# Expert weights through twelve ring slots and four staging slots that ScalarE and GpSimd empty by copies

## The reference, cut to what matters

```
g   = softmax(t @ rg_w + rg_b)             # one group of 4 is taken
e   = softmax(expert logits in the group)  # two experts of 8 are taken
hg, hu = t @ w_gate[e], t @ w_up[e]        # 2048 -> 512, for 32 experts
out = sum over chosen e of comb * ((silu(hg) * hu) @ w_down[e])   # 512 -> 2048
x   = LN2(alpha * x + gate2 * out)
```

## Time and profile before

| what | value |
|---|---|
| runs shown | 1637.08 us median of 3 (1636.77 to 1637.81) |
| the profiled execution | 1640.42 us |
| its span in the profile | 1638.6 us, 22796 instructions |
| TensorE (PE) busy | 1521.7 us, 93% |
| DVE, ScalarE (ACT), GpSimd (POOL) busy | 507.6, 253.9, 142.0 us |
| SP's queue, q1 | 510.20 MB, 78.4% of 16 engines over the span |
| chain that ended last | PE 78%, DMA 14%, DVE 3%, ACT 2% |

### The profile page before, as it was taken

The page is one execution under the profiler, slowest core; times in us unless marked ns, Lnnn a source line. Parts: engine busy times, 40 slices in busy tenths (PEclk is TensorE's granted clock), DMA queues, the critical chain, the costliest instruction groups (busy, mean ns, idle before and its releaser), DMA issues.

```text
span 1638.6 us, 22796 instructions
## 1 busy us (share of the span) xinstructions
PE 1521.7 (93%) x8535; PEld 659.9 (40%) x8536; DVE 507.6 (31%) x1446; ACT 253.9 (15%) x540; POOL 142.0 (9%) x215
## 2 busy tenths in 40 slices
PE   3999999999999899899999999999999999999974
PEld 2557555456344444433333333333333333333321
DVE  6468334323133246742111121212121121211216
ACT  2220000033122322112111110101010000000111
POOL 6001000041020140000000000000000000000011
PEclk9999899999799899799999999999999999999997
DMA  9995778883267869989999979999799999999965
GB/s 297 376 386 195 254 266 301 295 246 112 75 237 295 319 222 398 411 352 423 422 422 421 421 291 422 421 421 422 301 407 422 421 421 421 422 421 422 421 238 221
DMA packets 119288, 559.70 MB, mean 342 GB/s; under 512 B 15657, under 2 KB 20553, under 8 KB 64921
## 3 DMA queue, kind: packets, MB, share of 16 engines
q1 hardware_dynamic: 100800, 510.20, 78.4%
q0 software_dynamic: 17952, 46.05, 8.4%
q10 hardware_dynamic: 482, 2.70, 0.6%
HBM read 565.78 MB, written 42.37 MB: 371 GB/s over the span
## 4 chain that ended last, share of the span: by engine, by line
PE 78%; DMA 14%; DVE 3%; ACT 2%; issue 1%; POOL 0%; SPq 0%; POOLq 0%; DVEq 0%; ACTq 0%
PE bank L791 23%; PE bank L808 11%; DMA ring<-in_exp_w_up 10%; PE bank L2378 6%; PE bank L753 5%; PE bank L2286 5%; PE bank L2135 3%; PE bank L347 3%; DMA ring<-in_ada_w 3%; PE bank L2218 2%; PE bank L2329 2%; PE bank L760 2%; DMA ring<-in_w_in 2%; DVE BC L609 1%; PE bank L2113 1%
## 5 line engine op out<-in xcount | busy, mean ns | idle before, releaser
L791 PE MATMUL bank<-ring,BC 128*64 128x512 f32 x1984 | 473.4, 596 | 5.6 <-DMA ring<-in_exp_w_up 3.2
L791 PEld LDWEIGHTS bank<-ring,BC 128*64 128x64 f32 x1984 | 150.2, 137 | 301.8 <-issue 280.4
L808 PE MATMUL bank<-ring,BC 128*64 128x512 f32 x992 | 219.7, 595 | 16.7 <-ACT BC L714 16.7
L588 DVE COPY MOD<-bank 128x512 f32<-128x512 f32 x32 | 22.1, 692 | 430.2 <-PE bank L760 430.2
L753 PE MATMUL bank<-H,MOD 128*64 128x512 f32 x512 | 132.9, 592 | 0.3 <-DVE H L1995 0.3
L808 PEld LDWEIGHTS bank<-ring,BC 128*64 128x64 f32 x992 | 70.8, 137 | 142.5 <-issue 142.5
L544 POOL DMA_INDIRECT y_dram<-BC,y_row x31 | 29.9, 965 | 947.2 <-DVE y_row L618 862.1
L2378 PE MATMUL bank<-ring,MT 128*128 128x512 f32 x224 | 101.7, 607 | 1.0 <-issue 0.8
L702 ACT COPY MOD<-bank 128x512 f32<-128x512 f32 x32 | 18.7, 585 | 461.6 <-PE bank L760 461.6
L2286 PE MATMUL bank<-ring,MT 128*128 128x512 f32 x192 | 85.9, 600 | 1.0 <-ACT X L1211 1.0
L615 DVE COPY BC<-bank 128x512 f32<-128x512 f32 x31 | 21.4, 691 | 166.1 <-PE bank L808 166.1
(11 more groups left out here) (560 smaller groups left out, 1459.0 us busy)
## 6 DMA issues: line engine op xcount, KB each, us to landing
ring<-in_exp_w_gate SPq DMA_DIRECT2D x128, 1024.0 KB
ring<-in_exp_w_up SPq DMA_DIRECT2D x128, 1024.0 KB
ring<-in_exp_w_down SPq DMA_DIRECT2D x128, 1024.0 KB
ring<-in_ada_w SPq DMA_DIRECT2D x96, 1024.0 KB
ring<-in_w_in SPq DMA_DIRECT2D x20, 1024.0 KB
y_dram<-con POOLq DMA_DIRECT2D x20, 1024.0 KB, 34.2
ring<-in_w_out SPq DMA_DIRECT2D x16, 1024.0 KB
ring<-in_ssm_glu_w SPq DMA_DIRECT2D x4, 1024.0 KB
```

The lines of the kernel that those rows point to most:

```text
L791: mm = pe.matmul(bank[64 * i:64 * i + 64, 2, :], xT[:, q // 2, k % 4, 64 * (q % 2):64 * (q % 2) + 64], ring[:, at, 512 * (k % 4):512 * (k ...
L808: mm = pe.matmul(bank[64 * (c % 2):64 * (c % 2) + 64, 4 + c // 2, :], aT[:, j, :], ring[:, at, 512 * c:512 * c + 512], start=(j == 0), sto ...
```

## The change

Four more slots of one chunk, 12 to 15, are added to the ring. They take the place of memory that was `MT` and `GE`: slots 12 and 13 and the start of 14 lie in `MT`, the rest of 14 and slot 15 in `GE`. `HF` and `DW` move to other places for it. For every expert from 1 on, down chunk 8 to 11 is fetched into slot 12 to 15, before the expert's gate and up chunks. When TensorE has used the down chunk of the block before, an engine copies the staged chunk into its ring slot: ScalarE chunks 8 and 9, POOL chunks 10 and 11, POOL's one before and one after the scatter. Where the next block is of the same expert, the copy reads and writes the ring slot itself: the source is chosen by a register (`step`, 0 or 1, from a new part of `rint`). A staging slot may be filled again when the copy for the first block of the expert before has been made. TensorE waits for the copies instead of the landings. For expert 1 the order is 8, 9, 0, 1, 10, 11, 2 to 7, with a wait for `x1_ready` 2 ahead of chunk 10, as `GE` is in use until then. The DW products move to the start of DVE's tail. POOL's body for the block after the last also makes its two copies, and ScalarE waits for them before `y_all`.

```diff
--- before.py
+++ after.py
@@ build @@
+    stage_of = {j: RING + i for i, j in enumerate(STAGED)}
...
-        ring = sb("ring", [P, RING, 2048])
+        slots = sb("slots", [P, RING * 2048 + 2 * D + KD * T])
+        ring = slots[:, 0:(RING + len(STAGED)) * 2048].rearrange("p (s n) -> p s n", n=2048)
+        MTf, GEf = slots[:, RING * 2048:RING * 2048 + KD * T], slots[:, RING * 2048 + KD * T:]
...
-        DW = MTf[:, 2560:3328].rearrange("p (b i n) -> p b i n", b=3, i=2)
+        DW = BCf[:, 0:768].rearrange("p (b i n) -> p b i n", b=3, i=2)
...
+        def copy_staged(eng, copy, done, e, j, step, place):
+            at, to = slot_of[j], stage_of[j]
+            eng.wait_ge(used, len(plan) + (e - 1) * RING + j + 1)
+            eng.wait_ge(landed[at], 16 * (last_slot_uses[at] + 1) + 16 * place)
+            copy(ring[:, at:at + 1, :], ring[:, at:to + 1:to - at, :][:, bass.ds(step, 1), :]).then_inc(done, 1)
...
@@ moe_pool @@
             def body(e):
-                pool.wait_ge(S("rint_ready"), since("rint_ready") + 4)
+                step = pool.value_load(rint[0:1, bass.ds(e + (I_STEP - 1), 1)], min_val=0, max_val=1)
+                place = pool.value_load(rint[0:1, bass.ds(e + I_PLACE, 1)], min_val=0, max_val=E - 1)
+                copy_staged(pool, nc.gpsimd.tensor_copy, S("copied_pool"), e, 10, step, place)
+                pool.wait_ge(S("rint_ready"), since("rint_ready") + 5)
                 pool.wait_ge(S("y_row"), e)
                 pool.indirect_dma_start(...)
+                copy_staged(pool, nc.gpsimd.tensor_copy, S("copied_pool"), e, 11, step, place)
@@ moe_sp @@
-            with sp.Fori(1, E) as e:
+            def fetch(e, expert, before, j):
+                if j in STAGED:
+                    name, n = copies_of(j)
+                    sp.wait_ge(S(name), since(name) + before * 2 + n + 1)
+                    load_expert_chunk(sp, expert, j, live > e, stage_of[j])
+                    return
+                load_expert_chunk(sp, expert, j, live > e)
...
+            for j in (8, 9, 0, 1, 10, 11, 2, 3, 4, 5, 6, 7):
+                if j in STAGED:
+                    if j >= 10:
+                        sp.wait_ge(S("x1_ready"), 2)
+                else:
+                    sp.wait_ge(used, len(plan) + (first - 1) * RING + j + 1)
+                fetch(1, expert, 0, j)
+            with sp.Fori(2, E) as e:
                 first = sp.value_load(rint[0:1, bass.ds(e + I_FIRST, 1)], min_val=1, max_val=NBLK - 1)
+                before = sp.value_load(rint[0:1, bass.ds(e + (I_FIRST - 1), 1)], min_val=0, max_val=NBLK - 1)
                 expert = sp.value_load(rint[0:1, bass.ds(e + I_LIST, 1)], min_val=0, max_val=E - 1)
-                for j in range(RING):
-                    sp.wait_ge(used, len(plan) + (first - 1) * RING + j + 1)
-                    load_expert_chunk(sp, expert, j, live > e)
+                for j in [*STAGED, *range(8)]:
+                    if j < 8:
+                        sp.wait_ge(used, len(plan) + (first - 1) * RING + j + 1)
+                    fetch(e, expert, before, j)
@@ moe_dve, after the integer table's first four parts @@
+            go(V.tensor_scalar(places, bank[0:1, 3, 0:NBLK], E - 1.0, None, ALU.min))
+            V.tensor_tensor(rint[0:1, I_STEP:I_STEP + NBLK - 1], places[:, 1:], places[:, 0:NBLK - 1], ALU.subtract)\
+             .then_inc(S("rint_ready"), 1)
...
-            for b in range(3):
-                for i in range(2):
-                    V.tensor_scalar(DW[:, b, i, :], ident, cwt[:, b, i:i + 1], None, ALU.mult).then_inc(S("dw_ready"), 1)
@@ moe_act, body @@
                 turned_out(e + 1)
+                for j in (8, 9):
+                    copy_staged(act, nc.scalar.copy, S("copied_act"), e + 1, j, step, place)
                 act.wait_ge(used, len(plan) + (e + 1) * RING)
...
+            act.wait_ge(S("copied_pool"), 2 * (extra + FULL) + since("copied_pool") + 2)
             act.wait_ge(S("y_written"), 16 * (extra + FULL) + Y_FILLED)
@@ moe_pe, body @@
                     at = slot_of[8 + j]
-                    pe.wait_ge(landed[at], 16 * (last_slot_uses[at] + 1) + 16 * place)
+                    name, n = copies_of(8 + j)
+                    pe.wait_ge(S(name), since(name) + e * 2 + n + 1)
@@ tail_dve @@
+            for b in range(3):
+                for i in range(2):
+                    V.tensor_scalar(DW[:, b, i, :], ident, cwt[:, b, i:i + 1], None, ALU.mult).then_inc(S("dw_ready"), 1)
             dve.wait_ge(S("g2_ready"), 5)
```

More of the change, by code:

```diff
@@ L52 @@
 RING = 12
+STAGED = range(8, 12)
+STAGE_ACT = 2
 QC = 4
@@ L79 @@
 I_EXTRA, I_PLACE, I_LIST, I_FIRST = 0, 1, 1 + NBLK, 1 + 2 * NBLK
-I_LIVE, I_N = I_FIRST + E, I_FIRST + E + 1
+I_LIVE, I_STEP = I_FIRST + E, I_FIRST + E + 1
+I_N = I_STEP + NBLK
 def constants():
@@ L190 @@
     "slots_ready": ("sel_ready", 3),
-    "x_first": ("sel_ready", 4),
+    "copied_act": ("qs_ready", 8),
+    "copied_pool": ("glu_sig", 8),
 }
@@ L254, in build @@
         ones = con[:, C_ONE:C_ONE + P]
-        later = ring[:, 6:12, :].rearrange("p a b -> p (a b)")
+        later = slots[:, 6 * 2048:12 * 2048]
         Hf = H[:, :, :].rearrange("p a b -> p (a b)")
@@ L548, in body @@
                     .then_inc(S("y_written"), 16)
-            pool.wait_ge(S("rint_ready"), since("rint_ready") + 4)
+                copy_staged(pool, nc.gpsimd.tensor_copy, S("copied_pool"), e, 11, step, place)
+            for j in (10, 11):
+                pool.wait_ge(landed[slot_of[j]], 16 * (last_slot_uses[slot_of[j]] + 1))
+                pool.nop().then_inc(S("copied_pool"), 1)
+            pool.wait_ge(S("rint_ready"), since("rint_ready") + 5)
             expert_loops(pool, body, 1)
@@ L556, in moe_sp @@
             live = sp.value_load(rint[0:1, I_LIVE:I_LIVE + 1], min_val=1, max_val=E)
-            with sp.Fori(1, E) as e:
+            def fetch(e, expert, before, j):
[5 more added lines that the diff above has]
+                load_expert_chunk(sp, expert, j, live > e)
+            first = sp.value_load(rint[0:1, I_FIRST + 1:I_FIRST + 2], min_val=1, max_val=NBLK - 1)
+            expert = sp.value_load(rint[0:1, I_LIST + 1:I_LIST + 2], min_val=0, max_val=E - 1)
+            for j in (8, 9, 0, 1, 10, 11, 2, 3, 4, 5, 6, 7):
[6 more added lines that the diff above has]
+            with sp.Fori(2, E) as e:
                 first = sp.value_load(rint[0:1, bass.ds(e + I_FIRST, 1)], min_val=1, max_val=NBLK - 1)
+                before = sp.value_load(rint[0:1, bass.ds(e + (I_FIRST - 1), 1)], min_val=0, max_val=NBLK - 1)
                 expert = sp.value_load(rint[0:1, bass.ds(e + I_LIST, 1)], min_val=0, max_val=E - 1)
-                for j in range(RING):
-                    sp.wait_ge(used, len(plan) + (first - 1) * RING + j + 1)
-                    load_expert_chunk(sp, expert, j, live > e)
+                for j in [*STAGED, *range(8)]:
+                    if j < 8:
+                        sp.wait_ge(used, len(plan) + (first - 1) * RING + j + 1)
+                    fetch(e, expert, before, j)
             tail_sp(sp)
@@ L657, in moe_dve @@
             V.tensor_copy(rint[0:1, I_EXTRA:I_EXTRA + 1], behind[0:1, 0:1]).then_inc(S("rint_ready"), 1)
-            V.tensor_copy(rint[0:1, I_LIVE:I_N], behind[0:1, 1:2]).then_inc(S("rint_ready"), 1)
+            V.tensor_copy(rint[0:1, I_LIVE:I_STEP], behind[0:1, 1:2]).then_inc(S("rint_ready"), 1)
             V.tensor_scalar(rint[0:1, I_PLACE:I_FIRST], bank[0:1, 3, 0:2 * NBLK], E - 1.0, None, ALU.min)\
@@ L709, in body @@
             def body(e):
+                step = act.value_load(rint[0:1, bass.ds(e + I_STEP, 1)], min_val=0, max_val=1)
+                place = act.value_load(rint[0:1, bass.ds(e + (I_PLACE + 1), 1)], min_val=0, max_val=E - 1)
                 rows_out(e + 1)
@@ L720, in moe_act @@
             act.nop().then_inc(S("ys_act"), 1)
+            for j in (8, 9):
+                act.wait_ge(landed[slot_of[j]], 16 * (last_slot_uses[slot_of[j]] + 1))
+                act.nop().then_inc(S("copied_act"), 1)
             rows_out(0)
@@ L726, in moe_act @@
             nc.scalar.activation(rsm[:, 3, :, 0:1], rsm[:, 3, :, 0:1], ACT.Exp).then_inc(S("lg_exp"), 1)
-            act.wait_ge(S("rint_ready"), since("rint_ready") + 4)
+            act.wait_ge(S("rint_ready"), since("rint_ready") + 5)
             extra = expert_loops(act, body)
+            act.wait_ge(S("copied_pool"), 2 * (extra + FULL) + since("copied_pool") + 2)
             act.wait_ge(S("y_written"), 16 * (extra + FULL) + Y_FILLED)
```

15 lines of the change are left out of this document (7 added, 8 removed).

## The result

The changed kernel takes **1649.81 us** (median of 6 runs, 1644.63 to 1653.31), the kernel before in the same session 1636.92 (6 runs, 1635.76 to 1638.2): ratio 1.0082, interval 1.006 to 1.0103. So it is slower by 12.9 us on the medians; the forecast was 18.2 us more than 1637. The profiled execution took 1649.46 us with a span of 1647.7.

A forecast was written before the change was run, and what follows sets the result against it. TensorE was taken to set the pace at 28.15 us a block, with 14.7 us of waits for weights. Start 8.6, copies 3.0 and 3.2, end 3.4 gave +18.2 us; on the median 1637.08 that is 1655.3, taken as 1655, range 1646 to 1666.

The forecast's parts named there:

- B: Behind the two double blocks (one expert filling two blocks), the DMA waits for POOL's copy of chunk 11: 3.0 and 3.2 us.
- C: At the end, POOL's last copy lies wholly on the path to the first gather: +3.4 us.
- the copies are of another length: Sign of being wrong: POOL's copies in the profile after do not take about 3.1 us each.
- What bounds the kernel: In the expert loop TensorE sets the pace, 28.15 us a block; 14.7 us are waits for weights.
- The dips: Two falls in the GB/s row, 291 and 301, where no slot is given back; forecast to stay as deep.
- The fast rival: The holes at the double blocks are filled, both losses (1.6 and 13.1 us) vanish: 1625.8 us; chance 0.07.
- Term A: At the start, expert 2's gate/up chunks come later by two chunks net (5.1 us) and a dry stretch: +8.6 us.
- Waits and small parts: nothing: TensorE's waits for copies, the new integer operations, the value_loads and the moved DW products cost nothing.
- B1: Ahead of the second double block, the wait for POOL's copy behind the first one costs 3.0 us.
- B2: Behind the second double block, where the lead is already spent, the wait for POOL's copy costs 3.2 us.
- The likeliest case: The forecast itself for the whole kernel: +18.2 us, taken as 1655 us; chance 0.65.
- Half of it: Rival: the start costs only 5.1 us and POOL copies in 1.8 us: 10.7 us slower, 1648; chance 0.10.

The follow-up runs named there:

- gate16: Against the kernel before: sixteen slots, no copies, only chunks 0 to 3 of an expert have two places each; 1640.2 us, ratio 1.0018.
- a_late: The changed kernel with ScalarE's two waits moved from ahead of its first row copies to just ahead of the loop; 1646.19 us, ratio 1.0052.
- a_act4: a_late with ScalarE making all four copies and POOL none; 1650.33 us, ratio 1.0089.
- the ring of sixteen: Against the kernel before: sixteen slots as one ring in fetch order, no copies, TensorE's body standing four times; 1657.19 us, ratio 1.0131.

## Why the prediction was right, and where only its sum was

Direction and range were right, the range in part by luck. Of the terms one held roughly, one was put at nothing and cost 5.7 us at the start, and two (B and C) were far too large. One of the prediction's own signs of being wrong also came true: the copies are of another length.

- **What bounds the kernel, and that the slots bring nothing in steady state**: right. The dips stayed, the losses behind block 17 stayed, and the first loss came near block 5, as forecast. (In the earlier trace rows slice 30 has 407, which the reading "flat at 421 to 423" passed over; nothing hangs on it.) The fast rival is refuted by after and, for a different placing of the slots, by gate16. For the Trainium skill's rule (Perfetto Trace Analysis, Optimization Strategy), that consistent bubbles can mean too few buffers for the next tile, the trace does not agree here with the plain reading: two layouts with four more buffers (after and gate16) left the bubbles as long. What mattered was which buffer comes free next.
- **Term A, +8.6**: direction and place right, size too large. With a punctual start it measured 7.1: 1.0 for the two chunks that I took as free, 5.0 for the other two (5.1 taken), 1.1 for the wait, where I had a dry stretch of 3.4. In a_late, from the same timeline of SP, chunks 8 and 9 are issued at 696.68, 4.7 us behind the table and only 1.9 us ahead of chunk 0 (698.58). So they were not done before chunk 0, and their rest filled the time that I had counted as dry: when the wait ends there (707.31), the DMA's share has been 0.98 to 1.07 in every window of 1 us from 699 on. Why they are issued so late isn't shown. In after, with its late start, the gap does appear, but at 710 to 712 the share was still 0.42 and 0.23: the transfers issued before did not end together. That SP's wait ends at 711.36 where I had 711.8 is luck, since this trace reached the routing 4.0 us earlier and then lost 4.2 us; counted from the last gather I had 20.7, a_late has 20.0 and after 24.2. In after itself the loss up to block 8 grew by only 5.9, because TensorE started late.
- **"Waits and small parts: nothing"**: this step failed, for 5.7 us. I priced the waits in the loop's bodies and those of TensorE, and passed over the two that the diff puts ahead of ScalarE's `rows_out(0)`. What was queued behind them is the copy that TensorE waits for: it stood for 4.33 us ahead of L819 instead of 0.88, which is 3.5 of the 5.7. The rest, 2.2 us, is the clock. While TensorE stood, its granted clock fell to 0.50, the level of 1.2 GHz (1.00 over 689 to 691, 0.92 over 691 to 693, 0.50 over 693 to 695), and the eight matmuls of L819 took 1.98 us instead of 1.23. Over 695 to 702 it was 0.50 in after and 0.76 in before, and the first 16 matmuls took 6.42 us instead of 5.00. a_late gives all of it back at the start, and 3.7 us of it in the sum.
- **Terms B1 and B2, 3.0 and 3.2**: failed; 0.3 and 0.9 measured. Two steps were wrong. The copy takes 1.90 us, not 3.1, as the groups by line show, for POOL and ScalarE alike:

```profile
L543 POOL COPY slots<-slots 128x2048 f32 x62 | 118.0, 1903 | 800.5 <-PE bank L859 800.5
L543 ACT COPY slots<-slots 128x2048 f32 x62 | 114.7, 1896 | 55.5 <-PE bank L859 55.5
```

  I had scaled from the 128x512 copy by four (3.26), though the memset of the full tile (1.81) was the nearer row. And the copy of chunk 11 isn't what the DMA waits for. SP's last issue of the four (986.43 to 994.43) does follow that copy, which ends at 993.84, but transfers are in the queue: the DMA's share is 0.94 to 1.03 over 991 to 994. It is short of work at 986 to 989, about 0.8 us in all, behind ScalarE's copy of chunk 8. That POOL's copies cost nothing there agrees with a_act4.
- **Term C, +3.4**: failed; 0.45 measured. The timeline of POOL in after:

```profile
1596.96 0.97 POOL L562 DMA_INDIRECT y_dram<-BC,y_row  x1 [1.35 <-DVE y_row L660]
1597.93 1.91 POOL L543 COPY slots<-slots 128x2048 f32 x1
1601.90 1.12 POOL L887 DMA_INDIRECT slots<-y_dram,slot_i  x1 [2.07 <-issue]
```

  The gather waits for y_all, which ScalarE raises when the last scatter has landed: its next operation is at 1600.82, in the timeline of ScalarE,

```profile
1600.82 1.28 ACT L782 ACT_TABLE_LOAD   x1 [4.96 <-DMA y_dram<-BC,y_row]
```

  and the gather follows 1.1 us later. From the scatter's start to the first gather it is 4.94 us, before 4.49. The order is the same in before: there ScalarE's operation starts 3.36 us after the scatter's start (3.86 in after), and the gather 1.1 us later. I had read the 3.53 "issue" of the earlier trace rows as POOL's way out of the loop; it was the landing of the scatter and a signal, and all but 0.45 us of the copy lies beside it. The counter-test is a_act4, which has no copy on POOL: its scatter is followed by the gather after 4.50 us, as before. It has the longest tail all the same, because its YS copy, and so its scatter, is late.

The sum of 18.2 was thus 13.4, and 5.7 of the 13.4 come from waits that I had put at nothing. The likeliest case was not shown as it stood; the range held because errors of both signs met. Without the overlooked waits the kernel is a_late, with 9.6 us more by the sum and 1646.19 us, at the very edge of the range of 1646 to 1666. The rival "Half of it" (10.7) had the copy's length right (1.8), but it too has 5.6 us for B and C, where 1.7 were measured, and only 5.1 for A.

## What to carry to other kernels

When a change adds staging slots, work out with which transfer the queue resumes behind each hole, and when that one's slot comes free: slots that are tied to a kind of chunk move the hole instead of shortening it, and a chunk that is put ahead of the awaited ones, and for which there is no free time on the queue, is paid at the next point where the lead is spent. Go through the prologue (what an engine does once, ahead of the loop) as through the loop, wait by wait, and ask what is queued behind each: here two waits that only reported a landing cost 5.7 us at the start and 3.7 in all. And before a copy is put on a path through an "issue" gap, ask which signal ended the gap.

## What the runs showed of the hardware

- POOL and ScalarE copy 128x2048 floats within SBUF in the same time, 1903 and 1896 ns, although a 128x512 copy within SBUF took POOL 816 ns: four times the size took 2.3 times as long.
- With a body that stands four times, TensorE stood for 13.8 and 10.7 us of "issue" when each loop first returned to its head, and not again later. With half of the gate/up products standing three times there was no such stall. The page's rows of the instruction queues, of before, of the ring of sixteen and of gate16 in this order:

```profile
q14 instruction: 17, 0.14, 0.0%
```

```profile
q14 instruction: 31, 0.25, 0.0%
```

```profile
q14 instruction: 29, 0.24, 0.0%
```

  Both have more packets on this queue, by 14 and 12; only one of the two stalls. That the stall is the loading of instructions is my guess and isn't shown.
- A DMA stream that stopped didn't end at once: in gate16 the share falls over 961 to 964 as 0.45, 0.16 and 0.01, and in after it is still 0.42 and 0.23 at 710 to 712, where I had the queue dry. A count by the slowest engine gave the end of a long stretch well here, but overstated a short gap.
- A wait of 4.33 us of TensorE cost more than itself: the granted clock fell from 1.00 to 0.50 during it, and the matmuls behind it took 2.2 us longer than before.
